# Six edits in the first block of a two-block fp32 network: turning tokens before they are normalized, an earlier router fetch, halves without GpSimd, an earlier Silu table, and combining by columns

## The reference

```python
h = x                                              # (1, 256, 1024), fp32
h = h + gla_mixer(rms_norm(h, mix_norm[0]), ...)   # gated linear attention, 4 heads
h = h + swiglu(rms_norm(h, ffn_norm[0]), ...)      # dense, 2816 hidden features
h = h + swa_mixer(rms_norm(h, mix_norm[1]), ...)   # windowed attention, 16 heads
h = h + moe_swiglu(rms_norm(h, ffn_norm[1]), ...)  # router, 8 experts, top 2 of each token
out1 = rms_norm(h, final_norm)                     # the second block follows

def rms_norm(x, gain):
    y = x * rsqrt(mean(x * x, -1) + eps) * gain    # one factor per token, one gain per feature
def gla_mixer(...):                                # its last part
    o = o * rsqrt(mean(o * o, -1) + eps) * head_gain * silu(r)   # per head of 256 features
    return o @ w_out
def swiglu(h, wg, wu, wd):
    return (silu(h @ wg) * (h @ wu)) @ wd
def moe_swiglu(h, router, ...):
    logits = h @ router                            # 8 logits per token
    ...                                            # softmax over the best two
    out = out + combine[:, e:e+1] * swiglu(h, wg[e], wu[e], wd[e])
```

## Time and profile before

| | |
|---|---|
| time, median of 3 runs | 1750.78 us (1749.59 to 1751.77) |
| profiled execution: its time, its span | 1750.99 us, 1749.2 us |
| TensorE busy, share of the span | 1624.8 us, 93% |
| VectorE, ScalarE, GpSimd busy | 1229.8, 1039.2, 63.8 us |
| chain that ended last | TensorE 79%, VectorE 9%, ScalarE 7%, no wait shown 4% |
| mean granted TensorE clock | 0.967 |

### The profile page before, as it was taken

One profiled execution on the slowest core, in us unless ns is written; L12 is line 12 of the kernel. 1 busy time (PEld: TensorE's weight loads), 2 busy tenths in 40 slices (PEclk: granted clock), 3 DMA queues, 4 the chain that ended last, 5 costly groups with the idle time before them and its releaser, 6 DMA issues.

```text
span 1749.2 us, 21555 instructions
## 1 busy us (share of the span) xinstructions
PE 1624.8 (93%) x8649; PEld 1362.7 (78%) x8649; DVE 1229.8 (70%) x1298; ACT 1039.2 (59%) x1247; POOL 63.8 (4%) x64
## 2 busy tenths in 40 slices
PE   5997999988869999999999999999997989889987
PEld 5875888877758888888888888888886877788866
DVE  3655455357648888888888888888886566555665
ACT  4644444345537776777677777677676456454463
POOL 0000000011110000000000000000000200003000
PEclk9999999988969999999999999999998999899989
DMA  7422555552118999999999999999996643236410
GB/s 246 145 97 96 162 176 192 188 188 97 53 55 310 392 345 346 326 330 389 321 351 325 368 362 336 337 310 402 318 352 166 132 121 97 49 77 139 124 47 37
DMA packets 133080, 389.30 MB, mean 223 GB/s; under 512 B 8694, under 2 KB 14266, under 8 KB 132844
## 3 DMA queue, kind: packets, MB, share of 16 engines
q1 hardware_dynamic: 132692, 387.15, 65.4%
q10 hardware_dynamic: 280, 0.69, 0.1%
HBM read 386.77 MB, written 1.05 MB: 222 GB/s over the span
## 4 chain that ended last, share of the span: by engine, by line
PE 79%; DVE 9%; ACT 7%; issue 4%; DMA 0%; ACTq 0%; DVEq 0%; SPq 0%; POOL 0%
PE psum L354 25%; PE psum L356 24%; PE psum L355 23%; DVE wlo L189 4%; ACT whi L179 4%; PE psum L1493 1%; PE psum L1545 1%; DVE Ss L1192 1%; PE psum L413 1%; DVE mx L1197 1%; PE psum L2211 1%; PE psum L2197 0%; ACT hh L1604 0%; PE psum L2056 0%; ACT sil L1599 0%
## 5 line engine op out<-in xcount | busy, mean ns | idle before, releaser
L189 DVE TENSOR_TENSOR wlo<-raw,whi 128x2048 fp32r<-128x2048 f32 (+1 forms) x286 | 629.0, 2209 | 239.6 <-ACT whi L179 238.8
L179 ACT ACTIVATE whi<-raw 128x2048 fp32r<-128x2048 f32 (+1 forms) x286 | 526.3, 1847 | 250.7 <-PE psum L356 250.7
L354 PE MATMUL psum<-whi,xh 128*128 128x512 f32 (+1 forms) x1280 | 497.1, 388 | 15.9 <-DVE xl L2557 7.9
L356 PE MATMUL psum<-whi,xl 128*128 128x512 f32 (+1 forms) x1280 | 486.0, 380 | 0.0
L355 PE MATMUL psum<-wlo,xh 128*128 128x512 f32 (+1 forms) x1280 | 485.1, 379 | 0.0
L354 PEld LDWEIGHTS psum<-whi,xh 128*128 128x128 f32 x1280 | 242.3, 189 | 72.7 <-DVE wlo L189 12.6
L356 PEld LDWEIGHTS psum<-whi,xl 128*128 128x128 f32 x1280 | 242.0, 189 | 49.5
L355 PEld LDWEIGHTS psum<-wlo,xh 128*128 128x128 f32 x1280 | 242.5, 189 | 45.9 <-issue 0.2
L189 DVE TENSOR_TENSOR wlo<-raw_more,whi 128x2048 fp32r<-128x2048 f32 (+1 forms) x94 | 204.1, 2178 | 40.3 <-ACT whi L179 39.8
L179 ACT ACTIVATE whi<-raw_more 128x2048 fp32r<-128x2048 f32 (+1 forms) x94 | 171.3, 1827 | 53.8 <-PE psum L356 53.8
L354 PE MATMUL psum<-xh,whi 128*128 128x256 f32 (+2 forms) x552 | 164.5, 298 | 16.8 <-DVE wlo L189 15.2
(11 more groups left out here) (367 smaller groups left out, 1537.5 us busy)
## 6 DMA issues: line engine op xcount, KB each, us to landing
raw<-in_moe_w_down_dram SPq DMA_DIRECT2D x58, 1024.0 KB, 7.7
raw<-in_moe_w_gate_dram SPq DMA_DIRECT2D x43, 1024.0 KB, 6.3
raw<-in_moe_w_up_dram SPq DMA_DIRECT2D x41, 1024.0 KB, 6.1
raw_more<-in_moe_w_down_dram SPq DMA_DIRECT2D x30, 1024.0 KB, 7.8
raw<-in_w_in_dram SPq DMA_DIRECT2D x28, 1024.0 KB, 8.0
raw_more<-in_moe_w_up_dram SPq DMA_DIRECT2D x23, 1024.0 KB, 5.3
raw_more<-in_moe_w_gate_dram SPq DMA_DIRECT2D x21, 1024.0 KB, 6.7
raw<-in_moe_w_up_dram SPq DMA_DIRECT2D x23, 768.0 KB, 5.5
```

The lines of the kernel that those rows point to most:

```text
L179: act.e.activation(self.whi[:, i % self.ns, 0:kt * n], self.place[self.slots[i]][:, 0:kt * n], ACT.Copy, scale=1.0).then_inc(self.s_hi)
L189: dve.e.tensor_tensor(self.wlo[:, i % self.ns, 0:kt * n], self.place[self.slots[i]][:, 0:kt * n], self.whi[:, i % self.ns, 0:kt * n].bitca ...
L354: pe.e.matmul(o, lh, rh, start=start, stop=False)
L356: return pe.e.matmul(o, ll, rh, start=False, stop=stop)
```

## The change

1. **Head norm of gla in two parts.** The norm of the heads was formed once for all 256 tokens. It is now formed for the second 128 tokens (`head1`), then for the first (`head0`), each with its own squares, root and products `og`.
2. **Turning tokens from H.** In front of dense and of route, H itself is transposed (`turn_half`), and 1/rms of the token is applied later: as the scale of dense's Silu and of the product with `up`, and to route's eight logits. Groups k 0 to 3 are turned in the middle of the preceding product `out1` (it holds only the first 512 features), groups 4 to 7 behind the first piece of the next product. `xn` and its scaling go, in these two stages.
3. **Router.** Its 32 KB are fetched at the start of the kernel into `prm`, no longer in route. `xnh` is made from H by ACT with the scale 1/rms, `xnl` from H by DVE. GpSimd has no part in route. swa's two GpSimd memsets wait for the last of swa's `xl` (`x(7)`).
4. **Tables.** The Sqrt table for dense's end is loaded before the squares, and a Silu on one column stands ahead of the experts.
5. **The last conversion of a stage.** dense's `hi_to` and `lo_to` behind its last `down` piece go (`if p < 10`), and DVE's `lo_to` behind the last `down` piece of the last expert.
6. **Combining by columns.** The loops over halves and token groups change places, and a half is combined when its own `yl` is there.

```diff
-        OG = (0, 1, 4, 5, 2, 3, 6, 7)
+        OG = (4, 5, 6, 7, 0, 1, 2, 3)
+        OB = (5, 6, 7, 3, 4, 2)
...
+    def turn_half(pe, k, inst, ins_of, *free):
+        pe.wait_ge(*[h_added.at(inst, k // 4, j) for j in range(2)], *free)
+        for j in range(2):
+            ins = pe.e.transpose(psum[:, HB[k % 6], j * 128:(j + 1) * 128], H[:, j, k * 128:(k + 1) * 128], ident)
+        ins.then_inc(ins_of)
...
+            out1 = moving_steps(pe, "gla out1", [0, 128], [4, 5], y, [[y(4)], [y(6)]])
+            next(out1)
+            next(out1)
+            for k in range(4):
+                turn_half(pe, k, "gla", s_turn.end("dense", k), y(7))
+            run(out1)
...
+            for j in (1, 0):
+                srcs = [(psum[:, ob[j * 2 + h // 2], (h % 2) * 256:(h % 2) * 256 + 256], 128) for h in range(4)]
+                squares(act, f"head{j}", 8 + 4 * j, srcs, junk[:, j * 1024:(j + 1) * 1024], (o_acc, 1), crossed.at(2, 1 - j), *qb_at[0],
+                        *qb_at[1])
+                root(act, f"head{j}", st[:, 8 + 4 * j:12 + 4 * j])
...
             for half in range(2):
                 W.hi_to(act, P[f"gla out{half}"] + 1 + NS)
                 out_squares(act, "gla", half, TOK, bS[:, 0, 0:512], ("gla", half - 1))
+                if half == 0:
+                    act.wait_ge(W.passed(P["gla out1"]))
+                    high_by_gain(act, "dense", T, G_FFN[0], range(4), HB)
...
         def pool(pool):
-            pool.wait_ge(*dense.ends)
+            pool.wait_ge(*dense.ends, x(7))
...
-                W.lo_to(dve, P["ffn down"] + p + NS)
+                if p < 10:
+                    W.lo_to(dve, P["ffn down"] + p + NS)
...
+            for k in range(4):
+                logits(k)
+            for k in range(4, 8):
+                turn_half(pe, k, "swa", tr.end(k), *([xf_at(k - 6)] if k > 5 else []))
+            for k in range(4, 8):
                 ins = logits(k)
...
-        def pool(pool):
-            for j in range(2):
-                pool.wait_ge(*swa.ends, (n_hi, j + 1))
-                pool.e.tensor_tensor(xnl[:, j, :], xn[:, j, :], xnh[:, j, :].bitcast(F32), ALU.subtract).then_inc(n_lo)
...
+            for j in range(2):
+                dve.wait_ge((n_hi, j + 1), n_dve.at("moe", "rstd"))
+                dve.e.scalar_tensor_tensor(xnl[:, j, :], H[:, j, :], st[:, j:j + 1], xnh[:, j, :].bitcast(F32), ALU.mult,
+                                           ALU.subtract).then_inc(n_lo)
...
-                for j in range(2):
-                    for half in range(2):
+                for half in range(2):
+                    for j in range(2):
...
-                        pe.wait_ge(y_lo.at(e, 1), s_PT.at(g))
+                        pe.wait_ge(y_lo.at(e, half), s_PT.at(g))
...
             act.wait_ge(*route.ends)
+            act.e.activation(st[:, 60:61], st[:, 0:1], ACT.Silu, bias=0.0, scale=1.0).then_inc(s_silu)
...
             def down_(e, p):
-                S.lo_to(dve, down(e, p) + S.ns)
+                if (e, p) != (NE - 1, 10):
+                    S.lo_to(dve, down(e, p) + S.ns)
```

More of the change, by code:

```diff
@@ L311, in body @@
     W = Weights(sem, "w", pieces, slots, NS, whi, wlo, {i: raw[:, i, :] for i in range(RAW)})
-    NORMS = ["gla", "head", "dense", "swa", "moe", "meta0", "b0", "b1", "meta1", "end1", "end0"]
+    NORMS = ["gla", "head1", "head0", "dense", "swa", "moe", "meta0", "b0", "b1", "meta1", "end1", "end0"]
     SUMMED = ["dense", "swa", "moe", "b0", "b1", "meta1", "end1", "end0"]
@@ L319, in body @@
     TURNS = ["gla", "gla out", "dense", "swa", "b0", "b0 out", "b1", "b1 out"]
-    SCALED = ["gla", "dense", "swa", "moe", "b0", "b1"]
+    SCALED = ["gla", "swa", "b0", "b1"]
     s_xs = steps("scaled_by_dve", *[(x, h) for x in SCALED for h in range(2)])
@@ L741, in act @@
             act.e.activation(st[:, 44:45], st[:, 0:1], ACT.Sqrt, bias=0.0, scale=1.0).then_inc(s_table.end("gla", -1))
-            srcs = [(psum[:, ob[j * 2 + h // 2], (h % 2) * 256:(h % 2) * 256 + 256], 128) for j in range(2) for h in range(4)]
-            squares(act, "head", 8, srcs, junk, *across_at, *qb_at[0], *qb_at[1])
-            root(act, "head", st[:, 8:16])
-            high_by_gain(act, "gla out", T, G_HEAD)
+            for j in (1, 0):
[3 more added lines that the diff above has]
+                root(act, f"head{j}", st[:, 8 + 4 * j:12 + 4 * j])
+            high_by_gain(act, "gla out", T, G_HEAD, banks=OB)
             for half in range(2):
@@ L823, in dve @@
                 out_add(dve, "gla", half, TOK, done(f"gla out{half}", 2))
+                if half == 0:
+                    dve.wait_ge(W.passed(P["gla out1"]))
+                    low_by_gain(dve, "dense", T, G_FFN[0], range(4), HB)
         ends = [W.passed(P["gla out1"] + 1), s_table.at("gla", 1), h_added.at("gla", 1, 1), (s_one, 1)]
@@ L856, in pe @@
         def pe(pe):
-            pe.wait_ge(*gla.ends)
-            turn(pe, "dense", [(xn[:, j, :], 128, j * 128) for j in range(2)], scaled_at("dense"), {b: [] for b in range(8)})
             def turned(n):
                 for t in range(2):
-                    pe.wait_ge(f_hid.at(n, t), f_hl.at(n - 1, t) if n else x(2 + t))
+                    pe.wait_ge(f_hid.at(n, t), f_hl.at(n - 1, t) if n else x(4 + t))
                     for j in range(FC[n][1] // 128):
@@ L868, in pe @@
             for n in range(6):
-                run(moving_steps(pe, f"ffn gate{n}", [0, 128], [0, 1], x,
-                                 [[f_sil.at(n - 1, t)] if n else [] for t in range(2)], pieces_of(n)))
+                gate = moving_steps(pe, f"ffn gate{n}", [0, 128], [0, 1], x,
+                                    [[f_sil.at(n - 1, t) if n else h_added.at("gla", 0, t)] for t in range(2)], pieces_of(n))
+                if n == 0:
+                    next(gate)
+                    next(gate)
+                    for k in range(4, 8):
+                        turn_half(pe, k, "gla", s_turn.end("dense", k), *([x(k - 6)] if k > 5 else []))
+                run(gate)
                 if n:
@@ L899, in act @@
         def act(act):
+            high_by_gain(act, "dense", T, G_FFN[0], range(4, 8), HB)
+            root(act, "dense", st[:, 0:2])
             act.wait_ge(*gla.ends)
[L901 to L903 removed]
             def turned(n):
@@ L938, in dve @@
             invert(dve, "dense", st[:, 0:2])
-            scaled_dve(dve, "dense", xn)
-            low_by_gain(dve, "dense", T, G_FFN[0])
+            dve.wait_ge(*gla.ends)
             def turned(n):
@@ L1109, in pe @@
             run(moving_steps(pe, "swa out0", [0, 128], [0, 1], lambda k: o_lo.at(7), [[top.at(6, "scores")]] * 2))
-            run(moving_steps(pe, "swa out1", [0, 128], [4, 5], lambda k: o_lo.at(7), [[p_lo.at(7, 0)], [p_lo.at(7, 1)]]))
+            out1 = moving_steps(pe, "swa out1", [0, 128], [4, 5], lambda k: o_lo.at(7), [[p_lo.at(7, 0)], [p_lo.at(7, 1)]])
+            next(out1)
+            next(out1)
+            for k in range(4):
+                turn_half(pe, k, "swa", route_x.turned.end(k))
+            run(out1)
         def act(act):
@@ L1280, in pe @@
         def pe(pe):
-            pe.wait_ge(*swa.ends)
             def logits(k):
@@ L1875, in mid_sp @@
         sp.e.dma_start(c2[:, :], I["c2"]).then_inc(ld_c2, 16)
-    HALVES = [(j, half) for j in range(2) for half in range(2)]
+    HALVES = [(j, half) for half in range(2) for j in range(2)]
     U, xn0 = ox[:, 0:2, :], vvf[:, 0:2 * D].rearrange("p (j c) -> p j c", j=2)
@@ L2791, in _ @@
         Start.pool(pool)
-        for stage in (gla, swa, route):
+        for stage in (gla, swa):
             stage.pool(pool)
```

130 lines of the change are left out of this document (65 added, 65 removed).

## The result

The changed kernel took **1738.87 us** (median of 4 runs, 1737.73 to 1740.94), the kernel before 1750.18 us on the same chip (1749.05 to 1751.77). The ratio is 0.9931, with a 95% interval of 0.9919 to 0.9942: 11.3 us faster where my sum had 17.6. It lies inside my range, which ended at 1739.0, by 0.13 us; the interval of the ratio reaches beyond that end. That it lies inside is luck: the sum lacked most of one loss, and the width of the range came from other terms. The profiled execution has a span of 1739.1 us against 1749.2.

A forecast was written before the change was run, and what follows sets the result against it. TensorE, busy 93% of the span, was taken as the bound, winnable only where it idles or runs at half clock; 3.6 + 4.0 + 4.5 + 8.2 + 1.6 - 4.3 = 17.6 us gave a median of 1733.2 us, range 1728.5 to 1739.0.

The forecast's parts named there:

- Head norm: In front of gla's output product: the norm in two parts lets the transposes start earlier, gain 3.6 us.
- gla to dense: Handover from gla to dense, transposes moved into `out1` and behind the first gate piece: gain 4.0 us.
- dense to swa: Handover from dense to swa, without conversion, table load and memset in the way: gain 4.5 us, 0.8 of it clock.
- Route: Route up to the first gather, logits taken earlier and ranking not held by GpSimd: gain 8.2 us.
- Silu: First gather: the 1.28 us table load between its product and copy moves beside the branch, gain 1.6 us.
- Middle combines: Combines of the experts before the last one: nothing waits there, so no gain.
- Last combine: Last combine, where the first `yl` no longer stands behind VectorE's conversion: gain 0.7 us.
- The moved conversion: `dq`'s fifth group waits for the conversion behind `low(7)`: 3.0 us lost net, 1.3 of clock, 4.3 in all.
- The adds between gla and dense: Rival: `out1`'s two adds come over 2.3 us late and that handover's gain goes, 1737 us; chance 0.10.
- route gave 8.65 and not 5.5: Rival: route gives only the shorter norm, 5.5 us instead of 8.2, total 1736 us; chance 0.09.
- `dq` waited: Rival: `dq`'s fifth group does not wait, the last term becomes a gain of 0.7, 1728 us; chance 0.05.
- no gate waits in the experts: Rival: experts run against the weights' transfers, gains ahead are given back, 1755 us; chance 0.03.

The follow-up runs named there:

- e1: The changed kernel with VectorE's conversion of the last expert's last step back where it was, ahead of `yl`: 1727.44 us.
- e10: e1 with 16 and 12 products of constants, read by nobody, added in two of TensorE's waits in route: 1730.46 us.
- e7: e1 with two GpSimd subtractions of 128x1024, read by nobody, added beside VectorE's two `xnl`: 1732.42 us.
- e8: e1 without the Silu ahead of the experts: 1732.26 us.
- e3: The changed kernel with the call behind `low(7)`, which makes two conversions, placed between `low(3)` and `low(4)`: 1734.81 us.
- e2: The changed kernel with SyncE issuing the loads of the lambdas and of `c` ahead of the fetch into the freed buffer: 1731.81 us.
- e6: e5 with the loads of the lambdas and of `c` also issued ahead of the fetch, as in e2: 1727.71 us.
- e5: The changed kernel with the moved conversion alone between `low(3)` and `low(4)`, the next piece's left behind `low(7)`: 1728.01 us.
- e4: The kernel before with one edit alone, the last expert's last conversion on VectorE moved behind the eight `low(k)`: 1760.94 us.

## Why the prediction was right in direction and 6 us too hopeful

Term by term, against the table's steps:

- **Head norm**, 3.6 predicted: 3.41, with the transposes waiting for the sixth `og` as argued. (The "eight products" of a direction are eight records of four products; the times are right.)
- **gla to dense**, 4.0 (4.6 without a wait of `up`): 4.22. The slack of the two adds was 2.4 us (2.3 predicted), the idle inside the first gate 0.52 (0.5 predicted). `up` waits for nothing. This step carries some luck of the clock: in five other executions of the same instructions the lead behind dense was 6.5 to 7.8 us, here 7.6.
- **dense to swa**, 4.5, of which 4.0 to the transposes: 4.06, and 0.85 of clock behind them (0.8 predicted). That the 0.8 came so near is luck: the same idle of 3.35 us lowered the clock in seven profiled executions and left it at 1.00 in two, e1's and e10's. The 0.3 for a memset beside the conversion was nothing: the memsets run from 365.93 to 368.63, the first conversion starts at 367.14, 1.5 us of it beside them, and takes 2.29 us like any other. That is the pair that no row showed before. By the Trainium skill, SBUF — State Buffer, section Who interferes with whom, GpSimd that only writes doesn't hold a VectorE instruction with two SBUF inputs, and the trace agrees.
- **Route**, 8.2: 9.62 from the last add of swa to the first gather, less 0.97 by which the transposes inside `out1` had pushed that add back: 8.65. e7 shows the disputed part: GpSimd beside VectorE costs it 3.8 us here.
- **Silu**, 1.6: 1.36 to the second group; the row of e8 gives it back exactly.
- Together 22.9 us at that point, where the sum had 21.9.
- **The clock of the first gates** had no term. In the profiled execution it took 3.4 us back. It isn't the change's: five other executions of the same instructions up to there ended this stretch at 493.5, 493.9, 495.9, 495.9 and 504.1 us (e1, e3, e2, e6, e5). In four the clock had returned before the gates; in the changed kernel's and e5's it had not. The profiled execution is also the slowest of the changed kernel's four, 2.1 us over their median. I had taken one execution's stretch for a property of the kernel.
- **Middle combines**, nothing: nothing. **Last combine**, 0.7: 0.94.
- **The moved conversion** is the step that failed. Predicted: "It starts at 1342.85: 3.0 us lost, net of the 0.7", and up to 1.7 us of clock, 4.3 in all. The wait itself came as worked out (3.31; e1, e2 and e4 tie it to the move), and its clock. What I left out is the other reader of that instruction. Its end also frees the buffer, and on SyncE five loads stand behind the fetch that waits for it. I had asked what is queued behind it on VectorE and not on the queue that waits for its mark. That was 4.30 us of waiting and a second stretch at the half clock, 7 us by e2. Measured for the whole: 10.87 by the table, 9.7 by e4, 11.4 by e1, against 5.0 predicted: the 4.3, and the 0.7 that it was net of.

None of the rivals came true. The adds between gla and dense were 2.4 us early, route gave 8.65 and not 5.5, `dq` waited, and no gate waits in the experts: TensorE waits there for the placing matrices, 3.1 us as before. (The view of the earlier trace rows has one more row for before, 0.3 us for a `wlo`; it changes nothing.)

The profiled execution gained 10.1 us where the sum had 17.6: the last combine and the moved conversion together cost 5.8 more than it had, the clock of the first gates 3.4, against 1.0 more from the gains ahead and 0.7 at the end. The median, 2.1 us lower, gained 11.3. The range held the result, but not because its width stood for these: its slow end came from the adds' rival and from bounds of the clock. That was luck.

## What to carry to other kernels

Before an instruction is deferred, list everyone who waits for its mark: not only the consumer of its result, but whoever reuses its input's buffer, and everything behind that one in an in-order queue. Small loads that a later stage needs are safer ahead of the fetches that recycle buffers; it gave 7 us where a fetch was late, and nothing that could be measured where it wasn't (e6). A single execution's stretch at the half clock is not a fact about a kernel; and where TensorE waits a few microseconds in front of dense work, filling all but the last of the wait can pay: some 5 us here, while filling it beyond its end gave nothing.

## What the runs showed of the hardware that I had not expected

- Same instructions, different clock: the stretch at 0.50 around route lasted 17.1, 20.5, 20.5, 20.5, 27.3 and 27.3 us in six executions with the same program up to there (e3, e1, e2, e6, e5, changed).
- The clock stays at 1.00 across waits of 0.77 and 1.45 us that follow products of constants, where 6.24 to 7.15 us of idling in front of `dq` lowered it each time. An idle of 3.35 us in front of swa lowered it in seven executions and not in two (e1, e10), with the same instructions around it.
- GpSimd and VectorE, both with two SBUF operands, took turns in e7, an instruction at a time: 2.69 to 4.57 us and 4.65 to 6.63 us for two instructions each, and a VectorE instruction of 128x16 stood until GpSimd's ended.
- An f32 product of 128x256 is recorded as two instructions and takes 0.45 us at the full clock (twelve products stand as x24 in 5.34 and in 5.43 us).
